# Fetching the first half of x as two 64-row transfers, one issued by SyncE and one by ScalarE

## The reference

```
def rms_norm(x, g):
    y = x * rsqrt(mean(x * x, axis=-1) + EPS)
    return y * g
...
h = rms_norm(x, mix_norm_g)
proj = h @ w_in                    # 1024 x 2560: q, k, v and the two inputs of the recurrence
...
x = x + concat(norm(y_lru), norm(y_attn)) @ w_out
x = x + (gelu(gate) * val) @ w_down        # gate, val: convolved rms_norm(x) @ w_up
```

## Time and profile before

| what | value |
|---|---|
| median of 3 executions | 290.15 us (289.98 to 290.15) |
| the profiled execution | 290.13 us |
| its span, first to last instruction | 288.4 us |
| TensorE busy | 284.1 us (99%) |
| VectorE, ScalarE busy | 244.2 us (85%), 202.9 us (70%) |
| granted TensorE clock | 1.00 of full speed throughout |

### The profile page before, as it was taken

How to read it: one execution, slowest core, us unless ns; L and a number is a source line. 1 busy time by engine, 2 the same in 40 slices (tenths; PEclk the granted TensorE clock), 3 DMA queues, 4 the chain that set the end, 5 groups by cost and what they waited for, 6 DMA issues and landing times.

```text
span 288.4 us, 5012 instructions
## 1 busy us (share of the span) xinstructions
PE 284.1 (99%) x1642; PEld 246.6 (86%) x1642; DVE 244.2 (85%) x448; ACT 202.9 (70%) x389; POOL 11.4 (4%) x26
## 2 busy tenths in 40 slices
PE   8999999999999999999999999999999999999996
PEld 7688999898788999888888888888888888888885
DVE  2998898889999888999988788888888888888765
ACT  4893599999897687778676766667666666676540
POOL 3000004600000000000000000000000000000000
PEclk9999999999999999999999999999999999999999
DMA  7999950440365705375647474544647454100003
GB/s 276 428 419 419 398 186 7 148 145 14 134 228 209 257 38 164 130 291 166 278 145 287 148 261 177 160 162 152 252 145 291 145 181 178 77 0 0 0 0 145
DMA packets 8111, 52.23 MB, mean 181 GB/s; under 512 B 928, under 2 KB 1312, under 8 KB 2080
## 3 DMA queue, kind: packets, MB, share of 16 engines
q1 hardware_dynamic: 7920, 51.50, 48.1%
q0 software_dynamic: 176, 0.53, 0.5%
HBM read 50.98 MB, written 1.05 MB: 180 GB/s over the span
## 4 chain that ended last, share of the span: by engine, by line
PE 95%; DMA 2%; DVE 1%; ACT 1%; SPq 0%; issue 0%
PE bank L1419 25%; PE bank L1062 15%; PE bank L1063 14%; PE bank L1066 14%; PE bank L1423 13%; PE bank L1118 3%; PE bank L1372 3%; DMA x_tok<-in_x_dram 2%; PE bank L1383 1%; PE bank L1182 1%; PE bank L1306 1%; PE bank L1213 1%; PE bank L1222 1%; PE bank L1339 1%; PE bank L1176 1%; DVE w_hi L691 0%
## 5 line engine op out<-in xcount | busy, mean ns | idle before, releaser
L703 DVE TENSOR_TENSOR w_lo<-raw,w_hi 128x1024 fp32r<-128x1024 f32 x93 | 110.9, 1221 | 4.5 <-ACT w_hi L381 3.9
L381 ACT ACTIVATE w_hi<-raw 128x1024 fp32r<-128x1024 f32 x83 | 84.2, 1058 | 2.3 <-PE bank L1066 1.9
L1419 PE MATMUL bank<-h_both,w_hi 128*128 128x512 f32 x320 | 79.6, 391 | 0.0
L1419 PEld LDWEIGHTS bank<-h_both,w_hi 128*128 128x128 f32 x320 | 58.8, 188 | 11.3
L1423 PEld LDWEIGHTS bank<-h_both,w_lo 128*128 128x128 f32 x320 | 43.7, 191 | 3.1
L1423 PE MATMUL bank<-h_both,w_lo 128*128 128x256 f32 x320 | 44.7, 283 | 0.0
L614 ACT ACTIVATE tanh_a<-bank 128x256 f32<-128x256 f32 x44 | 16.7, 381 | 38.7 <-PE bank L1423 38.7
L1063 PE MATMUL bank<-w_lo,act_hi 128*128 128x512 f32 (+1 forms) x90 | 34.9, 388 | 0.0
L1062 PE MATMUL bank<-w_hi,act_hi 128*128 128x512 f32 (+1 forms) x90 | 34.9, 388 | 0.0
L1066 PE MATMUL bank<-w_hi,act_lo 128*128 128x512 f32 (+1 forms) x90 | 34.6, 385 | 0.0
L622 ACT ACTIVATE xc<-ygate,par 128x256 f32<-128x256 f32 x44 | 26.2, 596 | 4.2 <-DVE ygate L985 4.2
(11 more groups left out here) (193 smaller groups left out, 411.4 us busy)
## 6 DMA issues: line engine op xcount, KB each, us to landing
raw<-in_stream_dram SPq DMA_DIRECT2D x47, 1024.0 KB, 4.8
x_tok<-in_x_dram SPq DMA_DIRECT2D x2, 512.0 KB, 5.0
out_dram<-x_tok SPq DMA_DIRECT2D x3, 256.0 KB, 2.1
p_T<-in_gates_dram POOLq DMA_DIRECT2D x1, 512.0 KB, 9.5
out_dram<-x_tok SPq DMA_DIRECT2D x2, 128.0 KB, 2.0
par<-in_params_dram SPq DMA_DIRECT2D x1, 117.0 KB, 6.6
mix_g<-in_params_dram POOLq DMA_DIRECT2D x1, 4.0 KB, 5.6
```

The costliest lines, as they stand in the source:

```text
L381: act.activation(hi_tile(u)[:, :], raw_unit(u), ACT.Copy).then_inc(hi_done, 1)
L703: dve.tensor_tensor(w_lo[u % RING][:, :], raw_unit(u), hi_tile(u)[:, :].bitcast(F32), ALU.subtract).then_inc(lo_done, 1)
L1419: pe.matmul(acc[:, :], whi[:, kc, :], h_both[:, kc, :, :].rearrange("p b t -> p (b t)"), start=kc == 0, stop=False)
```

## The change

x's first half no longer comes as one transfer of 128 rows issued by SyncE. SyncE issues rows 0 to 63, and ScalarE issues rows 64 to 127 as the first instruction of its list, ahead of the table load. Both add 16 to x_landed[0], so the two places that wait for the first half (x_square on ScalarE and on VectorE) wait for 32. The second half, the weights and the parameters are issued as before.

```
+        X_LANDED = (32, 16)
...
         def _(sp):
             x_t = x[0].rearrange("(m p) d -> m p d", p=P)
-            sp.dma_start(x_tok[:, 0, :], x_t[0]).then_inc(x_landed[0], 16)
+            sp.dma_start(x_tok[0:HALF, 0, :], x_t[0][0:HALF, :]).then_inc(x_landed[0], 16)
             sp.dma_start(raw[0][:, :], stream[0]).then_inc(raw_landed[0], 16)
...
+            act.dma_start(x_tok[HALF:P, 0, :], x[0][HALF:P, :]).then_inc(x_landed[0], 16)
             act.wait_ge(consts, 1)
             act.activation(warm_out, eps, ACT.Sqrt).then_inc(warm, 1)

             def x_square(m, cols):
-                act.wait_ge(x_landed[m], 16)
+                act.wait_ge(x_landed[m], X_LANDED[m])
...
             def x_square(m):
-                dve.wait_ge(x_landed[m], 16)
+                dve.wait_ge(x_landed[m], X_LANDED[m])
```

## The result

The changed kernel is slower, by an amount outside the forecast range: median 291.10 us of 11 runs (290.80 to 292.60) against 290.11 us (289.98 to 290.16), ratio 1.0042 [1.0035, 1.0050]. The medians differ by 0.99 us, 0.34%. The profiled execution of the changed kernel took 290.88 us with a span of 289.1 us, 0.75 and 0.7 us more than before.

The account below looks back on a forecast made before the run. The prediction held that the end hangs on x's second half landing, then TensorE from 12.12 us. The issue term, -0.10 us, with all others 0, gave 290.03 from the profiled 290.13, or 290.05 us as median; range 289.7 to 290.75.

Parts of the forecast that it names:

- SyncE's first issue, 64 rows for 128: At the kernel's start, the issue takes 0.195 to 0.39 us; stream start moves by 0 to -0.195 us, taken as -0.10.
- Bytes and interleaving: x's first half: both queues start together, share the DMA engines one to one and finish when before; cost 0.
- The section on lateness: If ScalarE's transfer lags, x's first half is late by twice the lag up to 0.65 us, lag plus 0.65 beyond.
- Whatever moves TensorE's start: TensorE has almost no gap from 12.1 to 284 us, so moving its 12.12 us start moves the end by as much.
- The slack: Ahead of TensorE's transposes of the second half: about 0.5 us of first-half lateness is free, each further us costs one.
- The table load had its cover: ScalarE's table load moves back some 0.4 us within 1.75 us of idle time; cost 0.
- waiting for 32: Both x_square waits for the first half: 32 in place of 16 adds no instruction; cost 0.
- Rival 1: SyncE's issue time is fixed and nothing moves: second half lands at 8.51 us, time 290.15 us; chance a quarter.
- Rival 2: Two queues fill the stream's thin start at 1.8 us: -0.36 us, 289.79 us; chance one in ten.
- Rival 3: ScalarE's transfer late through table load or issues hindering each other: 291.55 us with load ahead; large lag one in eight.
- A lag of over 0.54 us: ScalarE's transfer starting that much behind SyncE's, where the loss passes 0.58 us (0.2%); chance one in eight.

Follow-up runs that it names:

- e1: Changed kernel with both 64-row halves issued by SyncE, one behind the other, ScalarE issuing nothing; 292.56 us.
- e8: Changed kernel with x's first half cut into even and odd rows, both transfers issued by SyncE; 293.05 us.
- e9: Changed kernel with x's first half cut into even rows issued by SyncE and odd rows issued by ScalarE; 290.65 us.
- e10: Changed kernel with the halves swapped: SyncE issues rows 64 to 127, ScalarE rows 0 to 63; 292.57 us.
- e6: Changed kernel cut by columns instead: 128 rows of 512 columns issued by SyncE, the other 512 columns by ScalarE; 290.14 us.
- e14: Changed kernel with an unequal cut: SyncE issues rows 0 to 95, ScalarE rows 96 to 127; 290.21 us.
- e7: Changed kernel with 14 warm-up products on TensorE in place of 11, transfers untouched; 291.07 us.
- e11: e5 with the gain mix_g issued by ScalarE in place of GpSimd; 290.74 us.
- e2: Changed kernel with ScalarE's half issued behind its table load and tiny root; 297.20 us.
- e13: Kernel before the change with the gain mix_g issued by ScalarE in place of GpSimd, behind the table load and tiny root; 289.82 us.
- e15: e13 with the parameters issued by SyncE behind raw5 in place of ahead of raw1; 291.28 us.
- e4: Kernel before the change with the parameters issued by ScalarE in place of SyncE, x's first half whole on SyncE; 291.39 us.
- e3: Kernel before the change with all 128 rows of x's first half issued by ScalarE, SyncE starting with raw0; 295.14 us.
- e12: Kernel before the change with the gain mix_g issued by ScalarE in place of GpSimd, ahead of the table load; 290.18 us.
- e5: Changed kernel cut by columns instead, two transfers of 128 rows by 512 columns, both issued by SyncE; 292.53 us.

## Why the prediction was wrong

**The step that failed.** "SyncE's first issue, 64 rows for 128" put the issue between 0.195 us (by rows) and 0.39 (fixed). It took 0.56 us, outside both ends, and lengthened the issue behind it from 0.42 to 0.56. The bounds came from transfers that all had 128 rows, and I took for given that fewer rows can't cost more; nothing in the trace said so. e1, e8, e9 and e10 show the 0.56 again, e6 and e14 don't. The packets begin 0.78 us behind the end of the issue here (2.15 against 1.37), where it was 0.64 us before the change (1.84 against 1.20). So the stream starts 0.31 us late, where -0.10 was forecast.

**The second one.** "Bytes and interleaving" had both queues start together at a cost of 0. They were issued together and started 0.77 us apart, and ScalarE's packets took 0.26 us instead of 0.168. The section on lateness had the case of a lag, but it held that "raw0 and all behind it land as before"; they landed 0.5 us late. For a lag of 0.77 us it gave 1.42 us of lateness; measured 1.09, of which 0.31 is the start.

**What makes up the 0.99 us.** e9 has the long issue and the late stream, with packets of 0.20 us for 0.26: 0.60 us over the kernel before, and TensorE's long stretch starts at 12.62 us. That is the stream's 0.5 us. The changed kernel's first half, on the chain through the lag and the slow packets, brings TensorE to 12.81. The two lie side by side and the later counts; 12.81 against 12.12 is the 0.7 us of the span. The medians differ by 0.3 us more than that. e7's profiled execution, with the same transfers, shows where such runs can differ: ScalarE's first packet begins at 3.25 us instead of 2.92, ScalarE starts on the first half at 5.44 us and TensorE on its long stretch at 12.99 us (span 289.3), at a clock of 1.00. Why this lag differs from run to run isn't shown.

**What was right.** Whatever moves TensorE's start moves the end as much: 12.12 and 288.4, 12.81 and 289.1, in e11 13.24 and 289.5, in e1 14.99 and 291.3, in e2 19.66 and 296.0, in e13 11.85 and 288.1; the difference is 276.3 us each time, within 0.1. (e15 is another matter: it lacks the parameters later on.) The slack was nearly right, 0.4 us for the 0.5 forecast: lateness of 0.64 (e14), 0.69 (e4) and 1.09 us (the changed kernel) moved TensorE by 0.22, 0.27 and 0.69, always some 0.4 us less. The table load had its cover, and waiting for 32 cost nothing (e6). Rival 1, nothing moves, is what e6 did and the change did not. Rival 2, a fuller start, didn't show: between 1.80 and 2.30 us e6 has 115 GB/s and the kernel before 123. Rival 3 was right in its place, a late first half that TensorE waits for, and wrong in its cause: the table load ran behind the issue, and the issues didn't hold each other up, as e1 has the same 0.56 us on one queue. The lag lay between the issue and the first packet. A lag of over 0.54 us had a chance of one in eight, and one of 0.77 us came.

The Trainium skill's page "DMA: Bandwidth & Descriptors" has in "Rules for kernel authors" that two transfers to disjoint partition halves serialize and that one 128-partition transfer is to be used. The advice held. But the page names no loss from such a cut, and its section "Issuing engines are not separate DMA queues" leaves issuing from a second engine a small saving of issue time; the runs make it neutral by columns (290.14 us) and at 96 and 32 rows (290.21), and a loss at 64 and 64 (291.10).

**Open.** Why the 64-row form, and not 96 and 32, takes 0.56 us to issue; why the second queue's first packet comes 0.77 us behind the first queue's in the changed kernel and in e3, but 0.17 us behind it in e6; why packets behind the first neighbouring rows are slow (the second transfer here and in e10, 0.24 us in e14) and those of interleaved rows are less so; the 0.2 us by which the stream is later than its start; the 0.7 us that e11 keeps.

## What to carry to other kernels

Bound the price of an unseen form of an instruction from above as well as from below: "less data, so at most the old price" wasn't safe by a factor of 1.4 here. When a transfer near the start is cut, look at the start and the time per packet of every stream behind it, not at the issuing engine; a DMA share of 1.0 hides whether packets became slower. And look at small transfers with short rows among the large ones that a kernel's start hangs on: moving one to another queue gained 0.26 us here, but only when it was issued at the right place (e13, and not e12).

## What the runs showed that I had not expected

- TensorE's granted clock fell to 0.50, that is 1.2 GHz, after it had been idle for 2.0 us (e10) or 2.08 us (e1), and it fell in e8 behind 1.42 and 1.50 us with eight transposes between them; four products then took 3.29 to 3.64 us instead of 1.96. In e5 it stayed at 1.00 behind 1.06 and 1.45 us. Of the changed kernel's 11 runs, with 1.49 us of idle time in the profiled one, one has a lowered mean clock of 0.994; of the five with three more warm-up products, none, which is too few to tell.
- The 32 packets of GpSimd's queue that carry the gain, 4 KB in all, go with a loss of 1.8 us in e5, where they fall among raw0's packets: e11 without them is that much faster.
- A DMA issue of ScalarE runs inside its own table load (0.94 us in e13, the load from 0.80 to 2.08).
- A transfer issued at 2.21 us on the second queue saw its first packet at 6.58 us (e2), with 1.36 MB of the first queue going by in 2.3 to 6.5 us.
